# Forgetting attention on one NeuronCore: P turned by plain transposes, 1/sum multiplied in when the output leaves PSUM

## The reference

```python
def forgetting_attention(q, k, v, dq, dk, qpos, kpos):   # in blocks of 128 queries
    s = q.k * d ** -0.5 + dq - dk            # D = cumsum(log f)
    s = where(kpos <= qpos, s, NEG_INF)
    p = softmax(s, axis=-1)                  # exp(s - max) / sum
    return p @ v
```

## Time and profile before

| | us |
|---|---|
| median of 3 runs (1830.89 to 1834.62) | 1833.17 |
| the profiled execution, span from its first to its last instruction | 1832.4 |
| TensorE busy in it | 1623.3 (89%) |
| VectorE busy | 971.5 (53%) |
| ScalarE busy | 595.1 (32%) |
| GpSimd busy | 776.0 (42%) |

### The profile page before, as it was taken

How to read it: one execution, slowest core, us unless ns; L and a number is a source line. 1 busy time by engine, 2 the same in 40 slices (tenths; PEclk the granted TensorE clock), 3 DMA queues, 4 the chain that set the end, 5 groups by cost and what they waited for, 6 DMA issues and landing times. The chain is left out here.

```text
span 1832.4 us, 27729 instructions
## 1 busy us (share of the span) xinstructions
PE 1623.3 (89%) x10719; PEld 1423.1 (78%) x10719; DVE 971.5 (53%) x1601; ACT 595.1 (32%) x1003; POOL 776.0 (42%) x925
## 2 busy tenths in 40 slices
PE   5789988999688867999699559999999997989997
PEld 2568887899466645899587459999999996878886
DVE  1561017640455533555425577887777776554543
ACT  2432133231344442222323334334343333332321
POOL 1431022321000007775113579999999993111211
PEclk7899999999799887788799779999999998999999
DMA  8335532220411048422322212222222223855662
GB/s 331 132 101 192 163 97 83 74 84 15 139 61 38 21 136 227 101 76 74 130 87 92 67 35 77 77 72 88 78 77 77 72 83 104 266 199 186 213 217 100
DMA packets 129382, 208.11 MB, mean 114 GB/s; under 512 B 38197, under 2 KB 86373, under 8 KB 125923
## 3 DMA queue, kind: packets, MB, share of 16 engines
q1 hardware_dynamic: 126786, 197.42, 33.1%
q10 hardware_dynamic: 2464, 8.91, 1.3%
HBM read 163.26 MB, written 42.91 MB: 113 GB/s over the span
## 5 line engine op out<-in xcount | busy, mean ns | idle before, releaser
L2695 DVE SCALAR_TENSOR_TENSOR fu_tmp<-fu_zp,fu_cw,fu_tmp 128x1024 f32<-128x1024 f32 x88 | 150.2, 1706 | 76.0 <-ACT fu_tmp L2630 74.5
L2936 PE MATMUL fd_ps<-fd_whi,fd_yhi 128*128 128x512 f32 x396 | 124.1, 395 | 18.0 <-DVE fd_wlo L2994 13.4
L2440 PE MATMUL fu_ps<-fu_thi,fu_wlo 128*128 128x272 f32 (+2 forms) x672 | 139.1, 288 | 0.0
L2440 PE MATMUL fu_ps<-fu_thi,fu_whi 128*128 128x272 f32 (+2 forms) x672 | 139.0, 288 | 0.0
L2440 PE MATMUL fu_ps<-fu_tlo,fu_whi 128*128 128x272 f32 (+2 forms) x672 | 138.9, 288 | 0.0
L2472 POOL TENSOR_TENSOR fu_wlo<-fu_s,fu_whi 128x512 fp32r<-128x512 f32 x84 | 120.2, 1442 | 19.2 <-ACT fu_whi L2586 18.8
L2956 ACT ACTIVATE fd_whi<-fd_w 128x1024 fp32r<-128x1024 f32 x65 | 68.8, 1060 | 175.9 <-PE fd_ps L2936 146.9
L2936 PE MATMUL fd_ps<-fd_wlo,fd_yhi 128*128 128x512 f32 x396 | 123.2, 392 | 0.0
L2586 ACT ACTIVATE fu_whi<-fu_s 128x512 fp32r<-128x512 f32 x84 | 50.8, 629 | 215.6 <-PE fu_ps L2440 89.7
L2440 PE MATMUL fu_ps<-h_hi,fu_whi 128*128 128x272 f32 (+1 forms) x504 | 105.6, 291 | 14.8 <-POOL fu_wlo L2472 14.8
L2472 POOL TENSOR_TENSOR fu_wlo<-w_up_raw,fu_whi 128x512 fp32r<-128x512 f32 x67 | 109.6, 1637 | 9.7 <-ACT fu_whi L2586 9.7
(11 more groups left out here) (366 smaller groups left out, 3901.7 us busy)
## 6 DMA issues: line engine op xcount, KB each, us to landing
fd_w<-in_w_down SPq DMA_DIRECT2D x65, 512.0 KB, 3.9
wa<-in_w_ada SPq DMA_DIRECT2D x24, 1024.0 KB, 5.7
w_up_raw<-in_w_up SPq DMA_DIRECT2D x88, 256.0 KB, 2.6
scr_y<-fu_tmp SPq DMA_DIRECT2D x22, 544.0 KB, 4.6
fd_y<-scr_y SPq DMA_DIRECT2D x44, 192.0 KB
fp_w<-in_w_fm SPq DMA_DIRECT2D x15, 512.0 KB, 3.6
scr_qkv<-fp_y SPq DMA_DIRECT2D x9, 512.0 KB, 2.9
dr_stg<-scr_qkv SPq DMA_DIRECT2D x8, 576.0 KB, 5.9
```

What stands on the lines that cost most here:

```text
L2440: last = pe.matmul(lane_of(q, o)[:, n, 0:size], w[:, o, kk], part(low, kk, slice(c, c + size)), start=(kk == 0 and m == 0), stop=(kk == HK ...
L2695: one = dve.scalar_tensor_tensor(yp, a, w, yp, ALU.mult, ALU.add)
L2936: last = pe.matmul(ps[OUT_BANK[p][n]][:, c:c + 512], y[:, k, n * P:(n + 1) * P], w[:, k, c:c + 512], start=(f == 0 and m == 0), stop=(f == ...
```

## The change

The diagonal `dg` is gone. TensorE turns unnormalised P by transposes against the identity. The reciprocals (in `st[..., 3]`) of a unit form one more group, WEIGHTS: two small products spread the column over 64 rows for each half, into a psT bank, and the group's emptying writes it to `bq`. VectorE multiplies the output by `bq` when it reads psO, into `ot`; ScalarE rounds `ot` to `h_hi` one step later, in even steps, and GpSimd subtracts for `h_lo`. The core of the diff:

```diff
@@ groups @@
+        WEIGHTS = 2
         for u in range(UNITS):
             for hh in range(2):
                 for b in range(0, u % NT + 1, 4):
                     groups.append((u, hh, b, min(4, u % NT + 1 - b)))
+            groups.append((u, WEIGHTS, 0, 1))
@@ def spread(eng, n) @@
+            if hh == WEIGHTS:
+                after(eng, o_set, 2 * (q - 1))
+                dst, src = bq[:, q % 2, (i % 2) * P:(i % 2 + 1) * P], psT[n % 2][:, 0, :]
@@ gpsimd @@
+            def lows(q):
+                pool.wait_ge(o_act, q + 1)
+                pool.tensor_tensor(K.h_lo[mixed(q)], ot[:], K.h_hi[mixed(q)], ALU.subtract).then_inc(o_lo, 1)
             for b in range(NBATCH):
                 ...
+                if b:
+                    pool.wait_ge(ca_q, H_C * (b + 1))
+                    lows(b - 1)
+                    pool.wait_ge(o_lo, b)
+            for q in range(NBATCH - 1, UNITS // 2):
+                lows(q)
@@ tensor, def turn(u) @@
                 for hh in range(2):
-                    pe.wait_ge(dg_set, 2 * u + hh + 1)
+                    pe.wait_ge(p_set, 2 * u + hh + 1)
                     ...
-                            last = pe.matmul(psT[n % 2][:, x, :], pb[:, u % 2, hh, (b + x) * P:(b + x + 1) * P], dg[:, u % 2, hh, :],
-                                             start=True, stop=True)
+                            last = pe.transpose(psT[n % 2][:, x, :], pb[:, u % 2, hh, (b + x) * P:(b + x + 1) * P], K.ident)
                         last.then_inc(t_mm, 1)
+                n = group_of[u, WEIGHTS, 0]
+                transposed(pe, n - 2)
+                pe.wait_ge(r_set, 2 * u + 2)
+                for hh in range(2):
+                    last = pe.matmul(psT[n % 2][rows_of[hh], 0, :], st[:, u % 2, hh, 3:4].broadcast_to([P, HD]), K.ident, start=True, stop=True)
+                last.then_inc(t_mm, 1)
@@ tensor, def values(q) @@
-                after(pe, o_dve, 2 * q)
+                after(pe, o_set, 2 * q)
@@ scalar @@
+                if u >= 2:
+                    act.wait_ge(t_mm, group_of[u - 2, WEIGHTS, 0] + 1)
                 act.activation(p, p, ACT.Exp, ...)
+            def high(q):
+                act.wait_ge(o_set, 2 * q + 2)
+                act.activation(K.h_hi[mixed(q)], ot[:], ACT.Copy).then_inc(o_act, 1)
-                if u >= 3 and u % 2 == 1:
-                    output(act, (u - 3) // 2, 0)
-                    output(act, (u - 3) // 2, 1)
+                if u >= 4 and u % 2 == 0:
+                    high((u - 4) // 2)
@@ vector @@
             def scale(u, hh):
                 dve.wait_ge(p_set, 2 * u + hh + 1)
-                chain.link(dve.reciprocal(st[:, u % 2, hh, 3:4], st[:, u % 2, hh, 2:3]))
-                dve.tensor_scalar(dg[:, u % 2, hh, :], K.ident, st[:, u % 2, hh, 3:4], None, ALU.mult).then_inc(dg_set, 1)
+                dve.reciprocal(st[:, u % 2, hh, 3:4], st[:, u % 2, hh, 2:3]).then_inc(r_set, 1)
+            def output(q, hh):
+                dve.wait_ge(pv_mm, 2 * q + hh + 1)
+                for u in (2 * q, 2 * q + 1):
+                    transposed(dve, group_of[u, WEIGHTS, 0])
+                after(dve, o_lo, q)
+                r = rows_of[hh]
+                dve.tensor_tensor(ot[r, :], psO[hh][r, 0:QC], bq[r, q % 2, :], ALU.mult).then_inc(o_set, 1)
```

More of the change, by code:

```diff
@@ L1020, in forgetting_attention @@
         st = sb("fa_st", [P, 2, 2, 4])
-        dg = sb("fa_dg", [P, 2, 2, P])
+        bq = sb("fa_bq", [P, 2, QC])
+        ot = sb("fa_ot", [P, QC])
         c16 = sb("fa_c16", [P, 2 * P], BF16)
@@ L1025, in forgetting_attention @@
         psO = [own.enter_context(nc.psum_tensor(f"fa_psO{i}", [P, 512], F32)) for i in range(2)]
-        c16_set, s_mm, at_chain, max_set, p_set, t_mm, pt_act, pt_dve, pv_mm, dg_set, o_act, o_dve = (
-            sem("fa_" + n) for n in "c16_set s_mm at_chain max_set p_set t_mm pt_act pt_dve pv_mm dg_set o_act o_dve".split())
+        c16_set, s_mm, at_chain, max_set, p_set, t_mm, pt_act, pt_dve, pv_mm, r_set, o_set, o_act, o_lo = (
+            sem("fa_" + n) for n in "c16_set s_mm at_chain max_set p_set t_mm pt_act pt_dve pv_mm r_set o_set o_act o_lo".split())
         nb_in = [sem("fa_nb_in0"), sem("fa_nb_in1")]
@@ L1073, in spread @@
             eng.wait_ge(t_mm, n + 1)
-            if q >= 2:
-                eng.wait_ge(pv_mm, 2 * (q - 2) + hh + 1)
-            dst, src = pt[:, hh, q % 2, b:b + size, (i % 2) * P:(i % 2 + 1) * P], psT[n % 2][:, 0:size, :]
+            if hh == WEIGHTS:
+                after(eng, o_set, 2 * (q - 1))
+                dst, src = bq[:, q % 2, (i % 2) * P:(i % 2 + 1) * P], psT[n % 2][:, 0, :]
+            else:
+                if q >= 2:
+                    eng.wait_ge(pv_mm, 2 * (q - 2) + hh + 1)
+                dst, src = pt[:, hh, q % 2, b:b + size, (i % 2) * P:(i % 2 + 1) * P], psT[n % 2][:, 0:size, :]
             if on_dve[n]:
@@ L1080, in spread, with mixed @@
                 eng.activation(dst, src, ACT.Copy).then_inc(pt_act, 1)
-        def output(eng, q, hh):
+        def mixed(q):
             j, m = q // (NT // 2), q % (NT // 2)
[L1085 to L1092, removed]
+            return slice(0, P), 5 + j, slice(m * QC, (m + 1) * QC)
         def mine(u, dve):
@@ L1262, in _ @@
                     exp_c(b)
+            high(UNITS // 2 - 1)
             act.wait_ge(ca_v, NBATCH)
@@ L1328, in _ @@
                 if u >= 3 and u % 2 == 1:
-                    output(dve, (u - 3) // 2, 0)
-                    output(dve, (u - 3) // 2, 1)
+                    output((u - 3) // 2, 0)
+                    output((u - 3) // 2, 1)
                 if step == 0 and 0 <= b < NBATCH:
```

## The result

The changed kernel takes 1868.94 us (median of 4 runs, 1861.79 to 1871.32); the kernel before, 1833.89 us (4 runs, 1830.89 to 1836.68). The ratio is 1.0183, 95% interval 1.0159 to 1.0206: slower by 35 us, where 20 were forecast. The profiled execution took 1868.46 us (span 1866.7 us); its span is 34.3 us longer than that of before's profiled execution (1832.4 us).

What follows compares the result with a forecast made beforehand. The prediction took a chain over VectorE and ScalarE to the psT emptying as the bound, TensorE itself with few tiles. It summed 1832.4 + 11.9 + 8 = 1852.3, so 1853 us as the median, range 1832 to 1880.

Steps and rivals of the forecast that it cites:

- What bounds the stage: Forgetting attention: a 3.3 us chain of maximum, exponential and bank emptying precedes the second half's turning; with few tiles TensorE bounds.
- Part 1: Turning of P by plain transposes: 216 tiles save 28 us of TensorE, a gain only where TensorE is not waiting afterwards.
- Part 2, the weights' group: Extra group through the psT banks, its product waiting for an emptying: +2.7 us (5 to 7 tiles), +7.7 us (1 to 4).
- Step 15: A step of 7 tiles: the weights' product ends at 577.75 instead of 577.56, +0.2 us.
- Step 12: A step with few tiles: VectorE empties group 0, and TensorE's next work starts at 553.3 instead of 552.37, +0.9 us.
- Step 9: A step with few tiles: ScalarE empties group 0 late, so P times V starts at 531.7 instead of 530.35, +1.35 us.
- Step 16, t = 8: One of three steps of eight tiles: the shorter turning wins 0.3 us in each, -0.9 us together.
- Part 3: The diagonal goes: 48 VectorE instructions of 287 ns less, counted as 0, with -3 in the range.
- Part 4: The output: GpSimd's subtraction 6 stands behind sample copies waiting for step 17, delaying VectorE's next maximum by 2.8 us, once.
- The sum at an unchanged clock: The stage's delays and gains without the clock: 2.7 + 7.7 - 1.3 + 2.8 = +11.9 us.
- Part 5, the clock: Longer TensorE gaps in nine steps of 5 to 7 tiles: about half bring a low clock, 5 x 1.7 = +8 us.
- The upper bound: Clock collapse: TensorE's work besides the turning, some 85 us, at half clock for half of it, +43 us; 1888, chance 0.10.

Runs made afterwards that it cites:

- the turning alone: The kernel before with plain transposes only, the diagonal still made and waited for, the division by the sum left out: 1835.05 us, ratio 1.0026.
- the filled version: The changed kernel with bf16 products that nobody reads, 10 between the halves (5 to 8 tiles), 6 ahead of each weights' wait: 1839.51 us, ratio 1.0055.
- the two-record version: The changed kernel with the turning again as fp32 products against the identity, two records a tile: 1848.57 us, ratio 1.0112.
- the control: The kernel before with only 10 filler products between the halves of units with 5 to 8 tiles: 1835.11 us, ratio 1.0028.
- bf16 products: The changed kernel with each transpose made an ordinary bf16 product of the upper halves of P's words, one record a tile: 1866.97 us, ratio 1.0205.
- the version with all three edits: The changed kernel with the weights' product in unused psO columns, banks emptied before the first exponential, subtraction before the sample copies: 1804.67 us, ratio 0.9869.
- the early emptying: The kernel before with ScalarE emptying the first half's psT banks ahead of its first exponential, VectorE keeping one group a unit: 1822.33 us, ratio 0.9948.
- turning alone, filled: The kernel before with plain transposes only, division left out, plus 10 filler products between the halves (5 to 8 tiles): 1827.29 us, ratio 0.9974.

## Why the prediction was right, and where it was not

The sign and the mechanism were right, and the time lies in the range (1832 to 1880), 16 us above the number. But the weights were not: the prediction had the longer chain as the larger part of the loss (11.9 us) and the clock as the smaller (8 us), and it is the other way round. By its steps:

- *What bounds the stage.* Right: the chain over the psT banks. Cutting it gained 8 us in the kernel before (9.4 in its stage), and halving the turning without that gained nothing.
- *Part 1.* The eight transposes elsewhere gave the right price: 14 take 0.94 + 0.96 us in step 15, seven in 0.94. TensorE's 28 us gave no time back, as forecast for the steps of 5 to 7 tiles, but "worth nothing" was too kind: the turning alone costs some 4 us (ratio 1.0026). Not all of the 28 us were off the path: with some two thirds of the added low clock filled away (0.86) the same version is 4 us faster than before (0.9974).
- *Part 2, the weights' group.* Right within 0.3 us in each of the four steps looked at. Step 15: +0.26, predicted +0.2. Step 12, where the next work began at 552.37, 2.39 us after the maximum:

```profile
562.43 0.82 DVE L1302 CUSTOM_DVE_ANT_0 fa_p<-fa_psS,fa_nb 128x640 f32<-128x640 f32 x1 [0.73 <-PE fa_psS L1161]
...
564.70 0.67 DVE L1085 COPY fa_pt<-fa_psT 128x512 f32<-128x512 f32 x1
565.43 0.44 PE L1177 MATMUL fa_psT<-cst,fa_st 128*64 128x128 f32 x4 [2.10 <-DVE fa_pt L1085]
565.79 0.43 PE L1211 MATMUL fa_psO<-ca_dg,ca_p 48*64 48x48 f32 x8
```

  565.79 - 562.43 = 3.36 us: +0.97, predicted +0.9. Step 9, 0.45 us before:

```profile
541.98 0.42 DVE L1302 CUSTOM_DVE_ANT_0 fa_p<-fa_psS,fa_nb 128x256 f32<-128x256 f32 x1
...
543.14 0.26 ACT L1087 ACTIVATE fa_pt<-fa_psT 128x128 f32<-128x128 f32 x1
543.45 0.44 PE L1177 MATMUL fa_psT<-cst,fa_st 128*64 128x128 f32 x4 [1.23 <-ACT fa_pt L1087]
...
543.98 1.30 PE L1190 MATMUL fa_psO<-fa_pt,vx 128*64 128x256 f32 x10
```

  543.98 - 541.98 = 2.00: +1.55, predicted +1.35. The product took 0.44 us with the tail of its last record, 0.36 to the next work; I had 0.25. Step 16, t = 8: from the start of the turning to the patch behind it 4.34 us (603.56 to 607.90), 4.55 before (581.18 to 585.73), -0.2, predicted -0.3.
- *Part 3.* No run tried the diagonal by itself. VectorE has 36 instructions fewer (48 diagonals less, 12 emptyings of weights more), and no row shows a gain from them in the kernel after.
- *Part 4.* Shown in two traces of step 17, not in a time. Against the earlier trace rows:

```profile
621.15 1.40 POOL L1140 COPY ca_q<-qkc 64x8 f32<-64x8 f32 x6 [28.24 <-PE fa_psO L1204]
...
622.63 0.72 POOL L1131 TENSOR_TENSOR h_lo<-fa_ot,h_hi 128x256 fp32r<-128x256 f32 x1
623.49 0.88 DVE L1319 TENSOR_TENSOR fa_ot<-fa_psO,fa_bq 64x256 f32<-64x256 f32 x2 [9.76 <-POOL h_lo L1131]
...
624.98 0.56 DVE L1302 CUSTOM_DVE_ANT_0 fa_p<-fa_psS,fa_nb 128x384 f32<-128x384 f32 x1
```

  The next maximum starts 2.9 us after the scores end (621.80 + 0.28), predicted +2.8. The 9.76 us beside the output are counted from VectorE's last work; only some 4 of them lie behind the end of P times V. With the subtraction ahead of the copies this delay is gone (experiment above). The subtraction took 0.76 us (mean of 12), predicted 0.7.
- *The sum at an unchanged clock,* +11.9: between 10 (the filled version) and 16 (the two-record version).
- *Part 5, the clock.* This is the term that was mis-sized: +8 predicted, 21 to 27 measured by the stage's rows (17 to 26 by the program's medians, each against its own runs of before). Its mechanism is shown by the filled version, which changes only what TensorE does while it waits (the added wait for the output's reading stood 2.3 us in all), together with the control, where the same kind of filler gains nothing. What failed is the count, "about half of these", five falls in the nine steps of t = 5 to 7. Read in stretches of 1 us, the low clock comes in 5 stretches behind 490 us before and in 14 after, and the longest, 567 to 584, stands right behind step 12 (t = 4): together with the short turning, the weights' wait opened a gap of 1 to 2 us in the short steps too (2.10 and 1.23 above), and there I priced only the delay. I had also taken the waits of 1.7 us without a fall as a sign that such waits are harmless, but in step 15 the engine turned for 1.8 us on either side of them, and now for 0.94; with the long turning back, the clock was at 0.91. (Nor were they all without a fall: in step 22 of the kernel before the clock was low from 631 to 636, behind a wait of 1.81 us that ended at 626.73 and one of 0.86 us that ended at 629.17.) The price of one was nearer: 21 to 27 us over 9 more stretches is 2.4 to 3 us each, above my 1.7; they are also longer (7 us in the mean, 5 before). The upper bound was a little low by its own reckoning: TensorE's work besides the turning was 156.5 - 61.9 = 94.6 us, not 85, which gives +47 instead of +43.

The Trainium skill ("TensorE: Matmul & The Clock Gate", Part 4, PE-mode transpose), which I gave the upper bound, is not what happened here: bf16 products gave 0.73 where transposes gave 0.75, and the version with all three edits, the same transposes with small gaps, ran at 0.90. Another section of that page ("A second HAM failure mode: psum-queue depth-cycling") fits: it says that TensorE, cycling through PSUM banks, stands idle for short times so often that its clock swings between the two levels. The waits of 46.8 us for a psT bank and the 0.75 agree with it; the filled version, 0.91 with the same banks and dependences, adds that it is the idleness, not the cycling.

## What to carry to other kernels

Work saved on an engine that waits afterwards is first of all idle time; on TensorE it can cost more than it saves, as the turning alone did here: 28 us less work at the full clock, and a clock of 0.79 instead of 0.90. So find the wait behind the work you shorten and remove that first (here: empty the bank before the exponential, keep a small extra product out of a two-bank ring), and only then shorten the work: the change was 1.8% slower with the waits, and with the waits taken out too the program was 1.3% faster (0.5% of it from the early emptying, which gains without the change). To price the clock's part of a loss, fill the gaps with products that compute nothing: what comes back is the clock's, what stays is the structure's and the fillers' own cost, for which a control is needed (4 to 5 us for 120 fillers here).

## What the runs showed of the hardware

- 216 TensorE records more, 22 us of work that computes nothing new, made the stage 21.5 us shorter (0.91 against 0.75).
- The granted clock did not fall in the gap: in step 15 TensorE stood still from 593.88 to 596.40, the stretch 596 to 598 was still at 1.00 and only 598 to 600 at 0.54. So here the turning right behind the gap took 0.96 us, as long as the one ahead of it, and P times V behind that paid.
- A 128x128 turning costs about 0.10 us a tile as a transpose of fp32 (seven in 0.94 us with the tail) and 0.23 us as two fp32 records.
- What follows the stage, the same code in every version, took 1178.1 us before and 1174.9 after, and in the other traces 1168.7 (bf16) to 1177.3 us (turning alone, filled). Before's trace is the longest of the twelve, so the 3.2 us are no effect of the change that these traces could show.
- Open: which of the unfilled steps keep the turning alone at 0.86.
